# Attention's weighted sums as three fp32r products, with a group's scores, turnings, exponentials, roundings and remainders interleaved tile by tile

## What is computed

```
def dsa_block(qpos, q_lat, q_idx, w_idx, c_kv, k_idx, topk):
    ...
    _, sel = lax.top_k(score, topk)
    kv_sel = jax.vmap(lambda c, i: c[i])(c_kv, sel)
    s = jnp.einsum('bqhc,bqkc->bqhk', q_lat, kv_sel).astype(jnp.float32) * (ATT_HEAD_DIM ** -0.5)
    ...
    p = jax.nn.softmax(s, axis=-1).astype(c_kv.dtype)
    return jnp.einsum('bqhk,bqkc->bqhc', p, kv_sel)
```

## Time and profile before

| what | us |
|---|---|
| time, median of 3 runs (lowest, highest) | 1017.39 (1017.03, 1017.8) |
| the profiled execution's own time | 1017.49 |
| its span in the trace | 1015.8 |
| PE busy | 996.9 |
| DVE busy | 714.0 |
| ACT busy | 493.8 |
| POOL busy | 118.1 |

### The profile page before, as it was taken

One profiled execution on the slowest core, in us unless ns is written; L12 is line 12 of the kernel. 1 busy time (PEld: TensorE's weight loads), 2 busy tenths in 40 slices (PEclk: granted clock), 3 DMA queues, 4 the chain that ended last, 5 costly groups with the idle time before them and its releaser, 6 DMA issues.

```text
span 1015.8 us, 18999 instructions
## 1 busy us (share of the span) xinstructions
PE 996.9 (98%) x7028; PEld 907.9 (89%) x7028; DVE 714.0 (70%) x1317; ACT 493.8 (49%) x868; POOL 118.1 (12%) x92
## 2 busy tenths in 40 slices
PE   9999999999999999999999999999999999999996
PEld 8999999999999988699765668889999999988886
DVE  6988888887322264699997523699989889942236
ACT  6656665566121264546346522576656665812121
POOL 0000000001121262045302205320000000000000
PEclk9999999999999999999999999999999999999999
DMA  7233332323223313132110102113323232333212
GB/s 252 84 100 107 102 105 90 116 80 105 86 86 111 113 44 116 36 123 82 44 42 1 43 1 83 43 42 126 124 83 124 85 121 96 125 103 101 98 57 84
DMA packets 30849, 90.48 MB, mean 89 GB/s; under 512 B 4689, under 2 KB 5329, under 8 KB 30801
## 3 DMA queue, kind: packets, MB, share of 16 engines
q1 hardware_dynamic: 30800, 89.83, 26.7%
HBM read 87.72 MB, written 2.10 MB: 88 GB/s over the span
## 4 chain that ended last, share of the span: by engine, by line
PE 81%; DVE 15%; ACT 2%; issue 1%; DMA 0%; SPq 0%; DVEq 0%; ACTq 0%
PE ps L1229 38%; PE ps L1287 22%; PE ps L1152 9%; DVE sc L2201 3%; DVE top L2200 3%; PE ps L1714 2%; PE ps L1424 1%; PE ps L1692 1%; DVE qk L2240 1%; PE ps L1705 1%; DVE wlo L1877 1%; PE ps L1489 1%; PE ps L1722 1%; PE ps L1337 1%; PE ps L1335 1%
## 5 line engine op out<-in xcount | busy, mean ns | idle before, releaser
L1229 PE MATMUL ps<-tsum,whi 128*128 128x264 f32 (+1 forms) x1280 | 243.1, 282 | 0.5 <-ACT ht L790 0.5
L1229 PEld LDWEIGHTS ps<-tsum,whi 128*128 128x128 f32 x1280 | 202.3, 188 | 0.7 <-issue 0.7
L1229 PE MATMUL ps<-tsum,wlo 128*128 128x264 f32 (+1 forms) x640 | 180.3, 282 | 0.0
L1229 PE MATMUL ps<-xh,whi 128*128 128x264 f32 (+1 forms) x480 | 135.4, 282 | 0.3 <-ACT sil L790 0.3
L1229 PE MATMUL ps<-xl,whi 128*128 128x264 f32 (+1 forms) x480 | 135.5, 282 | 0.0
L1229 PE MATMUL ps<-xh,wlo 128*128 128x264 f32 (+1 forms) x480 | 135.3, 282 | 0.0
L729 ACT ACTIVATE whi<-wraw 128x1408 fp32r<-128x1408 f32 (+1 forms) x48 | 74.6, 1555 | 123.0 <-PE ps L1287 123.0
L1787 DVE TENSOR_TENSOR wlo<-wraw,whi 128x1408 fp32r<-128x1408 f32 (+1 forms) x38 | 70.0, 1843 | 85.3 <-ACT whi L729 85.3
L1287 PE MATMUL ps<-hh,whi 128*128 128x264 f32 (+1 forms) x462 | 124.2, 323 | 0.0
L1287 PE MATMUL ps<-hh,wlo 128*128 128x264 f32 (+1 forms) x462 | 123.5, 322 | 0.0
L1287 PE MATMUL ps<-hl,whi 128*128 128x264 f32 (+1 forms) x462 | 123.4, 321 | 0.0
(11 more groups left out here) (287 smaller groups left out, 1828.0 us busy)
## 6 DMA issues: line engine op xcount, KB each, us to landing
wraw<-in_ffn_w_gate SPq DMA_DIRECT2D x43, 512.0 KB, 4.2
wraw<-in_ffn_w_up SPq DMA_DIRECT2D x42, 512.0 KB, 4.3
wraw<-in_ffn_w_down SPq DMA_DIRECT2D x32, 384.0 KB, 3.2
wraw<-in_ffn_w_down SPq DMA_DIRECT2D x32, 320.0 KB, 3.5
wraw<-in_w_in SPq DMA_DIRECT2D x19, 512.0 KB, 4.5
wraw<-in_w_out SPq DMA_DIRECT2D x8, 512.0 KB, 4.4
out<-zrow SPq DMA_DIRECT2D x8, 256.0 KB, 2.0
x<-in_x SPq DMA_DIRECT2D x3, 528.0 KB, 7.5
```

Of the source, the lines that this page charges most:

```text
L1229: mm = pe.matmul(ps[:, bank, 0:(HT, HALF_SEQ)[p // 2]], w[:, k * P:(k + 1) * P], v[:, k, :], start=(first and k == 0 and n == 0), stop=(k ...
```

## The change

The 28 weighings become split products. ACT rounds every turned tile out of PSUM (`weights_hi`, to `pt_h`), DVE subtracts that from PSUM (`weights_lo`, to `pt_l`), and PE makes three one-pass matmuls for a 128-key tile: rounded latents by rounded weights, the latents' remainder by rounded weights, and rounded latents by the weights' remainder. For the meta tile, 32 rows are turned instead of 16, the rounded rows lie at partitions 0 to 31 and the remainder at 32 to 63 of one tile, and two matmuls do: the latents' remainder over 16 rows, and one over 64 rows with a small tile `meta_c` that holds the rounded meta latents twice. The latents are split once: ACT rounds them (`chi`) right behind `ct`, and POOL makes the remainder `clo` and `meta_c` in `split_latents`, behind `mix_lo(9)`. `chi` and `clo` lie where `cs` was, `pts` where `v1` was, and the fourth score buffer moves to a row of `qk`.

Where a PSUM bank was free again after one copy, it is now free after both the rounding and the remainder, and the next turning into it waits for `pt_lo`.

In an iteration, the work of group G is no longer done in two halves but interleaved with the tiles of group G - 1. The mLSTM pieces and the late top-k rounds move to the ends of iterations.

```diff
-HEAD_GATED = ((1, 0), (1, 1), (2, 1), (3, 1))
-HEAD_HI = ((1, 1), (2, 0), (3, 0), (4, 0))
+HEAD_GATED = (1, 1, 2, 3)
+HEAD_HI = (2, 2, 3, 4)
...
-LATE_AT = ((4, 0), (4, 1), (5, 0))
+LATE_AT = (4, 4, 5)
...
-            cs = sb("cs", [P, NT, 256], F32, s)
+            with ExitStack() as c_scope:
+                cs = sb("cs", [P, NT, 256], F32, c_scope)
+            c_parts = sb("c_parts", [P, NT, 256], F32R, s)
+            clo, chi = c_parts[:, :, 0:LAT], c_parts[:, :, LAT:2 * LAT]
...
-            v1 = sb("v1", [P, NT, ML_H, VW], F32, s)
+            with ExitStack() as v_scope:
+                v1 = sb("v1", [P, NT, ML_H, VW], F32, v_scope)
+            pts = sb("pts", [P, NT * ML_H * VW], F32R, s)
+            meta_c = sb("meta_c", [64, LAT], F32R, s)
...
-        sbuf = [sil[:, 0, :], sil[:, 1, :], pt_flat[:, 1024:1024 + T], pt_flat[:, 1024 + T:1024 + 2 * T]]
+        sbuf = [sil[:, 0, :], sil[:, 1, :], pt_flat[:, 2048:2048 + T], qk[:, 3, :]]
+        pt_h = [pts[:, e * 512:(e + 1) * 512] for e in range(2)]
+        pt_l = [pts[:, (2 + e) * 512:(3 + e) * 512] for e in range(2)]
...
+                def split_latents():
+
+                    pool.wait_ge(c_hi, 1)
+                    pool.wait_ge(ct_turned, 1)
+                    pool.tensor_tensor(clo, cmat, chi.bitcast(F32), ALU.subtract).then_inc(c_lo, 1)
+                    m = N_META
+                    link(pool.memset(meta_c[:, :].bitcast(F32), 0.0))
+                    for e, r in enumerate((0, 32)):
+                        pool.wait_ge(c_lo, e + 1)
+                        pool.tensor_copy(meta_c[r:r + m, :], chi[0:m, 0, :].bitcast(F32)).then_inc(c_lo, 1)
+                    pool.wait_ge(c_lo, 3)
...
                 mix_lo(9)
+                split_latents()
                 causal_mask(3)
...
                 act.activation(ct[:, END[3]:T], ps[:, 5, 0:P], ACT.Copy).then_inc(ct_ready, 1)
+                act.activation(chi[:, :, :], cmat, ACT.Copy).then_inc(c_hi, 1)
                 hi(MIX0 + 4, 0, UW, False)
...
-                def copy_odd(G, tiles):
+                def weights_hi(G, tiles):
                     for i in tiles:
                         t = TP0[G] + i
-                        if t % 2 == 1:
-                            act.wait_ge(pt_turned, t + 1)
-                            if t >= 2:
-                                act.wait_ge(pv_step, t - 1)
-                            act.activation(pt_flat[0:ROWS[i], 512:1024], ps[0:ROWS[i], 1, :], ACT.Copy)\
-                                .then_inc(pt_odd, 1)
+                        R = META_ROWS if i == 0 else P
+                        act.wait_ge(pt_turned, t + 1)
+                        if t >= 2:
+                            act.wait_ge(pv_step, t - 1)
+                        act.activation(pt_h[t % 2][0:R, :], ps[0:R, t % 2, :], ACT.Copy).then_inc(pt_hi, 1)
 
                 late = None
                 for G in range(GROUPS + 1):
...
+                    last_tile = 1 + (G - 1) // 2
+                    if G < GROUPS:
+                        exps(G, (0, 1))
+                    if G >= 1:
+                        weights_hi(G - 1, (0, 1))
+                    if G < GROUPS:
+                        exps(G, (2,))
+                    if G >= 1 and last_tile >= 2:
+                        weights_hi(G - 1, (2,))
+                    if G < GROUPS:
+                        exps(G, (3,))
                     if G >= 1:
                         j, g = 1 + (G - 1) // 2, (G - 1) % 2
-                        copy_odd(G - 1, range(2, j + 1))
+                        weights_hi(G - 1, range(3, j + 1))
                         act.wait_ge(pv_step, TP0[G])
                         if G - 1 >= 2:
                             act.wait_ge(y_done, j - 1)
                         act.activation(olt[g], ps[:, 3, :], ACT.Copy).then_inc(ol_ready, 1)
+                        for h in range(ML_H):
+                            if HEAD_HI[h] == G:
+                                mlstm_hi(h)
...
-                        pe.wait_ge(pt_even if t % 2 == 0 else pt_odd, t // 2)
+                        pe.wait_ge(pt_lo, t - 1)
                     for q in range(4):
-                        mm = pe.transpose(ps[0:ROWS[i], t % 2, q * P:(q + 1) * P], pbuf[G % 2][:, q, START[i]:END[i]],
-                                          ident[:, :])
+                        k0, k1 = (START[i], END[i]) if i else (0, META_ROWS)
+                        mm = pe.transpose(ps[0:k1 - k0, t % 2, q * P:(q + 1) * P], pbuf[G % 2][:, q, k0:k1], ident[:, :])
                     mm.then_inc(pt_turned, 1)
 
                 def weigh(G, i):
                     t = TP0[G] + i
-                    pe.wait_ge(pt_even if t % 2 == 0 else pt_odd, t // 2 + 1)
-                    if i == 0 and G >= 1:
-                        pe.wait_ge(ol_ready, G)
-                    pe.matmul(ps[:, 3, :], cmat[0:ROWS[i], i, :], pt_flat[0:ROWS[i], (t % 2) * 512:(t % 2 + 1) * 512],
-                              start=(i == 0), stop=(i == 1 + G // 2)).then_inc(pv_step, 1)
+                    if i == 0:
+                        pe.wait_ge(pt_hi, t + 1)
+                        if G >= 1:
+                            pe.wait_ge(ol_ready, G)
+                        pe.wait_ge(c_lo, 3)
+                        m = N_META
+                        pe.matmul(ps[:, 3, :], clo[0:m, 0, :], pt_h[t % 2][0:m, :], start=True, stop=False)
+                        pe.wait_ge(pt_lo, t + 1)
+                        pe.matmul(ps[:, 3, :], meta_c[:, :], pt_h[t % 2][0:64, :], start=False, stop=False).then_inc(pv_step, 1)
+                        return
+                    pe.wait_ge(pt_hi, t + 1)
+                    pe.matmul(ps[:, 3, :], chi[:, i, :], pt_h[t % 2], start=False, stop=False)
+                    pe.matmul(ps[:, 3, :], clo[:, i, :], pt_h[t % 2], start=False, stop=False)
+                    pe.wait_ge(pt_lo, t + 1)
+                    pe.matmul(ps[:, 3, :], chi[:, i, :], pt_l[t % 2], start=False, stop=(i == 1 + G // 2)).then_inc(pv_step, 1)
...
...
+                    if G < GROUPS:
+                        scores(4 * G)
+                        scores(4 * G + 1)
+                    if G == 0:
+                        turn_mlstm((0, 1))
+                    if late is not None:
+                        project(late)
                     if G >= 1:
-                        for i in range(last_tile + 1):
-                            if 2 <= i + 1 <= last_tile:
-                                turn(G - 1, i + 1)
+                        turn(G - 1, 0)
+                        turn(G - 1, 1)
+                    if G < GROUPS:
+                        scores(4 * G + 2)
+                    if G >= 1:
+                        weigh(G - 1, 0)
+                        if last_tile >= 2:
+                            turn(G - 1, 2)
+                    if G < GROUPS:
+                        scores(4 * G + 3)
+                    if G >= 1:
+                        for i in range(1, last_tile + 1):
                             weigh(G - 1, i)
+                            if i + 2 <= last_tile:
+                                turn(G - 1, i + 2)
...
-                def copy_even(G, tiles):
+                def weights_lo(G, tiles):
                     for i in tiles:
                         t = TP0[G] + i
-                        if t % 2 == 0:
-                            dve.wait_ge(pt_turned, t + 1)
-                            if t >= 2:
-                                dve.wait_ge(pv_step, t - 1)
-                            dve.tensor_copy(pt_flat[0:ROWS[i], 0:512], ps[0:ROWS[i], 0, :]).then_inc(pt_even, 1)
-
+                        dve.wait_ge(pt_hi, t + 1)
+                        if i == 0:
+                            ins = dve.tensor_tensor(pt_h[t % 2][32:32 + META_ROWS, :], ps[0:META_ROWS, t % 2, :],
+                                                    pt_h[t % 2][0:META_ROWS, :].bitcast(F32), ALU.subtract)
+                        else:
+                            ins = dve.tensor_tensor(pt_l[t % 2], ps[:, t % 2, :], pt_h[t % 2].bitcast(F32), ALU.subtract)
+                        ins.then_inc(pt_lo, 1)
+
+                def late_rounds(G):
+                    for n, at in enumerate(LATE_AT):
+                        if at == G:
+                            select(4, LATE_ROUND + n, LATE_ROUND + n + 1)
 
                 for G in range(GROUPS + 1):
                     last_tile = 1 + (G - 1) // 2
...
+                    if G < GROUPS:
+                        masked(4 * G)
+                        masked(4 * G + 1)
                     if G >= 1:
-                        copy_even(G - 1, range(2, last_tile + 1))
+                        weights_lo(G - 1, (0, 1))
+                    if G < GROUPS:
+                        masked(4 * G + 2)
+                    if late is not None:
+                        normalise(late)
+                    if G >= 1 and last_tile >= 2:
+                        weights_lo(G - 1, (2,))
```

(57 more changed lines are left out.)

13 lines of the change are left out of this document (1 added, 12 removed).

## The result

The changed kernel takes 1032.5 us (median of 4 runs, 1032.37 to 1032.77), the kernel before 1017.21 in the same session (4 runs, 1016.85 to 1017.8): a ratio of 1.0151, interval 1.0137 to 1.0166. The profiled execution took 1032.77 us with a span of 1031.1. So it is slower, as forecast, but by 15.3 us where the sum said 10.4, and it lies at the upper edge of the range.

The account below looks back on a forecast made before the run. PE was taken to bound attention, busy 67.75 of 70.52 us. The sum: 1017.49 + 10.0 (attention) + 0.45 (POOL's subtraction) + 0 (ACT's rounding of the latents) = 1027.9 us, range 1019.5 to 1032.5.

Parts of the forecast that it names:

- The ladder: Attention: masks, exponentials, roundings and remainders make DVE and ACT wait in turn; 9.6 us of steps in iteration 6; chance 0.73.
- the walked 80.3 us: Attention's iterations 0 to 8, added up step by step through the three engines' instruction lists: 80.3 us against 70.52 before.
- The forecast's 10.0 more: Attention's predicted loss, taken between +9.8 against the measured 70.52 us and +10.2 against the walked lists of before.
- 6.4 less work, 16.4 more waits: PE in attention: 3.2 us saved on 20 tiles and 3.2 on 8 meta tiles, against 16.4 us more waits.
- the 0.2 that the forecast put on top: Attention: the iterations' sum gave +9.8 us, the forecast took +10.0.
- The longest losers: Sign in the trace: iterations 5 (10.84 to 13.5 us) and 6 (9.19 to 12.2 us) would lose most.
- PE busy near 62: Sign in the trace: PE busy near 62 us in an attention stretch near 80 us; before, 67.75 in 70.52.
- Ahead of attention: Latents' split before attention: 0 us for ACT's rounding, 0.45 (0 to 1.5) for POOL's subtraction; first scores 0.4 to 0.5 later.
- The pair at 474: Two DVE multiplications ahead of attention, 5.37 us together, held until POOL's remainder ends; would still end near 479.8.
- PE stays the bound: Rival in attention: DVE and ACT keep up, PE's waits stay at 2.8 us; 1011.6 us, faster; chance 0.07.
- half of the waits: Rival in attention: some added steps overlap, 8.2 us of waits instead of 16.4; 1019.8 us; chance 0.13.
- More than the ladder: Rival in attention: POOL's reading also blocks DVE's remainders, one block of up to 4.6 us; 1032.6 us; chance 0.07.

Follow-up runs that it names:

- rounds_first: The changed kernel reordered: PE scores all four heads first, ACT rounds tiles 0 and 1 before the exponentials, DVE's remainders stand behind later masks; 1016.01 us.
- act_first: The changed kernel with one edit: ACT rounds tiles 0 and 1 ahead of the exponentials of heads 0 and 1; 1025.25 us, ratio 1.0078 to the kernel before.
- warm: The changed kernel with extra matmuls on PE, adding nothing to the results, wherever it waited over 0.5 us in attention; 1029.32 us.
- act_first_warm: The act_first kernel with extra matmuls on PE ahead of tile 3's weighing in iterations 5, 6 and 7; 1023.64 us, beside 1024.54 for act_first run again.
- front_only: The kernel before with only the latents' rounding on ACT and their subtraction on POOL added, results not used; 1017.86 us, ratio 1.0004.
- warm_late: The changed kernel with extra matmuls on PE in iterations 5 to 7 alone; 1030.7 us, ratio 1.0127 to the kernel before.
- split_only: The split products of the change in the order of the kernel before; 1033.84 us, ratio 1.0156 to the kernel before.

## Why the prediction was right in sign and short in size

- **The ladder** was right, and is the cause. The trace has its steps (2.88 for 2.89, third mask to fourth; 3.59 for 3.49, second to third), rounds_first takes it away with the same instructions and 16.5 us of the time go, and act_first takes one rung away and 8.1 us of stretch go. With the clock held up (warm), the walked 80.3 us measure 82.25.
- **The step that failed: the granted clock was put at nothing.** Every duration was taken at full speed, since before the clock was never below 1.00 in attention. In the changed kernel it fell to half four times, for 3.4 us each. The last waits over 1 us ahead of the falls are 1.02, 1.21, 1.41 and 1.65 us; a wait of 1.21 at 606 us had no fall behind it. The four falls cost 3.9 us by warm, and one 1.2 by act_first_warm. The forecast's 10.0 more, 1.7 that warm has above it (82.25 - 70.52 = 11.7) and 3.9 are the 15.67 of the stretch, to 0.1. The Trainium skill ("TensorE: Matmul & The Clock Gate", A second HAM failure mode: psum-queue depth-cycling) describes a kernel in which short idle times between groups of matmuls make the clock swing between its two levels. The trace agrees with 0.50 and 0.51, and this was the rule to weigh in the forecast: a change whose effect is many waits on PE.
- **The second step that was off: "6.4 less work, 16.4 more waits".** The price of a pass, 0.23 us from the output product, holds in a weighing for a pass that waits for nothing and stands behind another pass; the first pass behind a turning takes 0.31 to 0.33. But the meta tiles give 1.7 instead of 3.2, and in tiles whose rounding or remainder comes just in time the passes wait for it. In rounds_first these short waits cost about the 3.2 that the 128-key tiles were to save. The profile counts them as busy, so that its idle time grew by 10.5 us (2.8 to 13.25) and not by 16.4. The sum of both, which the walk gives, is 2.0 us short in warm (1.7 with the 0.2 that the forecast put on top). What makes these 2.0 is not shown: the steps of the walk hold the wait for the last tile's remainder already (0.73 and 0.23, against 0.73 and 0.34 in the trace), and warm has its extra matmuls besides.
- **Iterations.** "In iteration 6 ACT and DVE take turns" is what the timelines show, and PE's wait before tile 3 (1.65) is put to ACT's rounding, that before the meta tile too. The longest losers were to be 5 and 6; 6 lost 4.1, but 2 (2.7) lost more than 5 (2.3), and 7 (2.2) came near, with the clock at 0.88 in 2 and 0.89 in 7. With the clock held up (warm) the order is as forecast: 6 loses 3.2, 5 loses 2.7, 2 loses 1.9.
- **PE busy near 62** was wrong: 72.94. Up to 6.4 of it is half clock, and what is left, 66.5, is near the 66.40 of rounds_first: 61.4 as forecast, 1.5 of the meta tiles, about 3 of short waits counted as busy, and some 0.5 that stays open.
- **Ahead of attention.** The pair at 474 ended with POOL's remainder, at 479.3, so that ACT's rounding of the latents cost nothing there; the TENSOR_SCALAR lost 0.52 (0.43 forecast). The first scores came 0.10 later than before, not 0.4 to 0.5, but this profile was already 0.43 ahead before the added instructions; from there the delay is 0.53, and 0.51 in front_only. This part was right.
- **The rivals.** *PE stays the bound* and *half of the waits* fell with the ladder. *More than the ladder* would give 1032.6 and so nearly the measured time, but by a block that isn't there. In rounds_first a remainder starts inside POOL's subtraction of the output weight (start, us, engine, line, what):

```profile
571.17 4.55 POOL L641 TENSOR_TENSOR wlo<-wraw,whi 128x2048 fp32r<-128x2048 f32 x1
...
574.71 0.68 DVE L2408 TENSOR_TENSOR pts<-ps,pts 128x512 fp32r<-128x512 f32 x1
```

It takes 0.68 us, as everywhere. The Trainium skill ("SBUF — State Buffer", Who interferes with whom) says, as the forecast had it, that a DVE instruction with one input in SBUF, outside the two-port modes, does not contend with GpSimd; the trace agrees with these 0.68 us.

## What to carry to other kernels

When a tile needs one engine and then another, write the order of both engines as one chain, with its steps from the trace, before counting busy time: here the same instructions took 86 or 69 us of stretch, by the order alone, at 63% and 54% busy on the two engines. Then ask what the waits do to PE: if an engine that never paused begins to wait a microsecond at many places, price its work there at half clock for a few microseconds as well. And don't read a saving off busy time alone: compare the start of a matmul with the end of what it depends on. Here a third pass that came 0.39 behind the second instead of 0.23 was waiting for a remainder, and the profile showed no idle time for it.

## What was not expected of the hardware

- The granted clock fell to half behind waits that made up a small part of the time: in the change before 592.99 the longest is 1.65 us, and PE is busy for 10.88 of the 13.31 us of that iteration. Each fall in it lasted 3.4 us, but one of 6.8 and one of 10.2 us were seen too (warm_late, split_only), and in one kernel profiled twice (act_first) the one fall stands in two different places.
- Passes of 128x512 in one accumulation start 0.23 us apart in the output product. In a weighing of the change the third starts 0.39 behind the second in 7 of 20 tiles and 0.23 or 0.24 in the other 13. In all seven it starts 0.06 behind the end of its remainder on DVE; in the other 13 the remainder ended 0.09 us or more before. So it is a wait, with no idle time shown. What makes the first pass behind a turning take 0.31 to 0.33 was not tried, and stays open.
- A DVE TENSOR_SCALAR of 128x400 took 0.87 and 0.89 us beside POOL's subtraction in two kernels, against 0.37 without it.
